# A twelve-stage fp32 transformer kernel on one core: later squares in the first stage, and layer norms that take the mean from a bank of its own

## The chip, the core and the metric

The kernel runs on one core of a Trainium2 chip. That core has TensorE (matrix products, PE in the rows), VectorE (DVE), ScalarE (ACT), GpSimd (POOL) and SyncE (SP), which here issues nearly all the transfers. Each engine works through a list of instructions of its own, in order, and semaphores connect the lists. The metric is the device time of one execution, in microseconds.

## The reference

A batch of one, 256 tokens, width 1024. The first block has two layers: gated feed-forward pieces (stages f0 to f3), a mixer (m0, m1) and a cross attention (c0, c1), each behind an RMS norm. The second block has two layers: a mixer (b0, b1), a feed-forward piece (f4, f5), and a layer norm behind each of them.

```python
def swiglu(h, w_gate, w_up, w_down):
    return (jax.nn.silu(h @ w_gate) * (h @ w_up)) @ w_down

mix = jnp.concatenate([o_gla, o_rwkv, o_nsa], axis=-1) @ w_out[l]
x = _layer_norm(DEEPNORM_ALPHA * x + mix, ln1_w[l], ln1_b[l])
ffn = (jax.nn.silu(x @ ffn_w_gate[l]) * (x @ ffn_w_up[l])) @ ffn_w_down[l]
x = _layer_norm(DEEPNORM_ALPHA * x + ffn, ln2_w[l], ln2_b[l])
```

## The kernel before, in words

The state x lies with its features on the partitions, as eight blocks k of 128 features by 256 tokens. Products are near fp32: every operand is split into a high part of the type fp32r and a rest. For a weight unit of 128x1024 (eight tiles of 128x128), ScalarE writes the high part `w_hi` (L148, `act_split`) and VectorE the rest `w_lo` (L159, `dve_split`); TensorE then runs, for each tile, a product of 512 columns with `w_hi` (high part and rest of the activations side by side) and one of 256 columns with `w_lo`. These two are called a pair below. Where the high part and the rest of the activations are multiplied apart there are three products of 256 columns, a triple.

Weights come through a ring of six slots (`ring`) and are split into four slots of `w_hi` and `w_lo`. A transfer waits until the slot's last unit has been split, a split until the unit four before it has been used by TensorE.

The order is written out by hand. Each stage has a list of pieces, and every engine goes through the same list and does its share of each piece (`pe_program`, `act_program`, `dve_program`, `pool_program`). Splits are put between the pieces: in `f` stages each unit as early as `can_split` allows, in the mixers where the strings of `WEAVE` have a dot (high part) or a comma (rest). In these strings z is a warm-up product (`pe_warm`: the identity times itself into an idle bank, result unused) and m the next piece of the output chain, with the layer norm at its end.

What the change touches:

- Stage f0. Pieces x0 to x8 make the high part and rest of the activations h (`act_x`, `dve_x`). GpSimd squares x and adds the squares up (`pool_x`: eight squares and six additions into `rows`). `pe_rs` sums them over the partitions (piece rs 0, products `ps<-consts,rows`), VectorE takes the root (`dve_rs`), and piece rs 1 spreads it over the partitions (`ps<-consts,stats`). Gate j of side h is eight pairs; the first one, j = 0, is done for both sides together, block by block. The column sums of rs 0 stand before its last block.
- The layer norm (`pe_ln`, `act_ln`, `dve_ln`, `pool_ln`, pieces from `ln_pieces`) is run behind b0, f4, b1 and f5. Piece x adds a block of the result, ld centres it by a mean over the first half (VectorE) and squares it (ScalarE), GpSimd adds the squares up. Piece ls sums x and the squares over the partitions into the two halves of one bank; ScalarE squares the mean, VectorE subtracts (`rows<-ps,rows`), ScalarE takes logarithm and exponential for the reciprocal root R, and VectorE writes the mean M (`scratch<-ps`). Piece lm subtracts M from blocks 0 and 1 on VectorE and from blocks 2 to 7 on GpSimd (`x<-x,scratch`). Piece lx multiplies a block by R (`x<-x,rows`), ScalarE writes the high part `h` with gain and bias and the new x, VectorE writes the rest (`h<-x,h`). For blocks 1, 4 and 7 (`vector_norm`) VectorE writes the new x. The next stage's first products need, block by block, the rest.

## Time and profile before

| | us |
|---|---|
| median of 3 runs | 2079.61 |
| lowest and highest run | 2076.35, 2083.39 |
| span of the profiled execution (first to last instruction) | 2076.2 |
| TensorE, matmuls busy | 1971.9 |
| VectorE busy | 1512.7 |
| ScalarE busy | 1117.3 |
| GpSimd busy | 408.7 |

The profiled execution has no time of its own beside its span; the fastest run is 0.15 us above that span, so what lies around the span is taken as small, and the median run is 3.4 us above it. Times within the trace count from the first instruction. A busy matmul time has modelled ends, since matmuls overlap.

### The profile page before, as it was taken

How to read it: one execution, taken by the hardware profiler on the slowest of the kernel's cores; microseconds unless marked ns; L12 is line 12 of the kernel's file. 1: busy time of each engine (PE TensorE's matmuls, PEld its weight loads, DVE VectorE, ACT ScalarE, POOL GpSimd, SP SyncE). 2: the span in 40 equal slices, each digit the busy share in tenths (PEclk: the TensorE clock that was granted, in tenths of full speed). 3: DMA queues.
4: the chain of work that ended last, by engine and by line, in shares of the span. 5: the costliest groups of instructions: out<-in, count | busy, mean ns of one | idle time of the engine just before them, and what ended most of it. 6: DMA issues, size and time to landing. Idle time of an engine off the chain costs nothing.

```text
span 2076.2 us, 32905 instructions
## 1 busy us (share of the span) xinstructions
PE 1971.9 (95%) x12512; PEld 1721.6 (83%) x12512; DVE 1512.7 (73%) x2649; ACT 1117.3 (54%) x2048; POOL 408.7 (20%) x371
## 2 busy tenths in 40 slices
PE   7999999999999999899999998899998999899997
PEld 6888888888888888698888977588887878688886
DVE  6976776787678767777876688577766687677765
ACT  5654565565455556655554543456554543456554
POOL 3521002222112210023220101102213012112213
PEclk9999999999999999999999998999999899999999
DMA  7556533355556555044555440225555240234652
GB/s 252 190 178 196 168 132 116 121 191 178 179 192 194 182 185 182 32 153 165 188 180 186 141 134 1 87 93 174 191 183 177 85 135 30 77 113 151 191 183 85
DMA packets 88718, 309.83 MB, mean 149 GB/s; under 512 B 9840, under 2 KB 11632, under 8 KB 88176
## 3 DMA queue, kind: packets, MB, share of 16 engines
q1 hardware_dynamic: 88272, 305.03, 44.9%
q10 hardware_dynamic: 288, 2.69, 0.4%
q8 instruction: 100, 1.64, 0.3%
q14 instruction: 58, 0.48, 0.1%
HBM read 306.63 MB, written 1.05 MB: 148 GB/s over the span
## 4 chain that ended last, share of the span: by engine, by line
PE 81%; DVE 10%; ACT 4%; issue 3%; POOL 1%; DMA 1%; SPq 0%; DVEq 0%; ACTq 0%; POOLq 0%
PE ps L134 79%; DVE scratch L159 3%; ACT scratch L148 2%; PE ps L139 2%; DVE w_lo L159 2%; DVE stats L176 1%; DVE scratch L165 1%; POOL rows L159 1%; DVE scratch L186 1%; DMA ring<-in_w 1%; ACT w_hi L148 1%; ACT L153 0%; DVE scratch L171 0%; DVE stats L159 0%; DVE x L159 0%
## 5 line engine op out<-in xcount | busy, mean ns | idle before, releaser
L134 PE MATMUL ps<-h,w_hi 128*128 128x512 f32 (+1 forms) x2912 | 900.2, 370 | 25.2 <-DVE w_lo L159 16.3
L159 DVE TENSOR_TENSOR w_lo<-ring,w_hi 128x1024 fp32r<-128x1024 f32 (+3 forms) x573 | 699.0, 1230 | 302.8 <-ACT w_hi L148 299.7
L148 ACT ACTIVATE w_hi<-ring 128x1024 fp32r<-128x1024 f32 (+3 forms) x573 | 584.3, 1029 | 419.3 <-PE ps L134 413.9
L134 PE MATMUL ps<-h,w_lo 128*128 128x256 f32 x2512 | 708.5, 282 | 0.0
L134 PEld LDWEIGHTS ps<-h,w_hi 128*128 128x128 f32 x2912 | 530.2, 192 | 124.3 <-issue 21.0
L134 PEld LDWEIGHTS ps<-h,w_lo 128*128 128x128 f32 x2512 | 481.3, 192 | 0.0
L134 PE MATMUL ps<-f,w_hi 128*128 128x512 f32 (+1 forms) x1444 | 417.7, 355 | 0.1
L134 PE MATMUL ps<-f,w_lo 128*128 128x256 f32 x1184 | 331.2, 280 | 0.0
L159 POOL TENSOR_TENSOR f<-f_work,f 128x256 fp32r<-128x256 f32 x132 | 185.1, 1403 | 557.4 <-ACT f L148 557.3
L134 PEld LDWEIGHTS ps<-f,w_hi 128*128 128x128 f32 x1444 | 254.4, 189 | 41.9 <-issue 0.4
L134 PEld LDWEIGHTS ps<-f,w_lo 128*128 128x128 f32 x1184 | 223.8, 189 | 0.1
L134 PE MATMUL ps<-scratch 128*128 128x128 f32 (+8 forms) x1696 | 200.1, 319 | 15.2 <-DVE scratch L159 7.1
L134 PEld LDWEIGHTS ps<-scratch 128*128 128x128 f32 (+3 forms) x1696 | 162.5, 181 | 50.7 <-issue 16.4
L185 ACT ACTIVATE scratch<-ps 128x512 f32<-128x512 f32 (+9 forms) x196 | 91.2, 485 | 188.2 <-PE ps L134 149.9
L159 POOL TENSOR_TENSOR rows<-x 128x256 f32<-128x256 f32 x64 | 52.8, 826 | 481.6 <-DVE x L159 472.4
L159 DVE TENSOR_TENSOR f_work<-f_work,ps 128x256 f32<-128x256 f32 x306 | 126.7, 415 | 6.7 <-ACT f_work L185 6.6
L159 DVE TENSOR_TENSOR f_work<-f_work 128x256 f32<-128x256 f32 x264 | 113.7, 431 | 8.6
L134 PE MATMUL ps<-w_hi,h 128*128 128x512 f32 (+2 forms) x384 | 112.5, 369 | 1.9 <-DVE w_lo L159 1.5
L185 ACT ACTIVATE f_work<-ps 128x256 f32<-128x256 f32 x306 | 111.2, 366 | 1.3 <-PE ps L134 1.3
L139 PE MATMUL ps<-consts,scratch 128*128 128x128 f32 (+3 forms) x428 | 70.1, 296 | 31.0 <-DVE scratch L165 14.9
L159 DVE TENSOR_TENSOR scratch<-scratch 128x512 f32<-128x512 f32 (+7 forms) x108 | 70.3, 678 | 35.3 <-ACT scratch L185 27.4
L148 ACT ACTIVATE scratch<-ps,stats 128x256 f32<-128x256 f32 (+3 forms) x143 | 68.9, 497 | 47.0 <-PE ps L134 25.1
(158 smaller groups left out, 2048.1 us busy)
## 6 DMA issues: line engine op xcount, KB each, us to landing
ring<-in_w SPq DMA_DIRECT2D x518, 512.0 KB, 3.8
ring<-in_w SPq DMA_DIRECT2D x48, 384.0 KB, 3.6
ring<-in_w SPq DMA_DIRECT2D x16, 396.0 KB, 3.2
ring<-in_w SPq DMA_DIRECT2D x8, 256.0 KB, 5.4
stage_consts<-in_ctwo ACTq DMA_DIRECT2D x1, 1346.0 KB, 6.2
stage_consts<-in_cthree ACTq DMA_DIRECT2D x1, 1283.0 KB, 5.7
x<-in_x SPq DMA_DIRECT2D x4, 256.0 KB, 6.9
scratch<-in_m SPq DMA_DIRECT2D x1, 1024.0 KB, 10.5
```

Source lines behind the costliest of these rows:

```text
L134: return self.e.matmul(out, lhsT, rhs, start=start, stop=stop, skip_group_check=free)
L139: return self.e.transpose(out, x, self.K.ident[0:x.shape[0], 0:x.shape[0]])
L148: return self.e.activation(out, x, func, **k)
L159: return self.e.tensor_tensor(out, a, b, op)
L165: return self.e.tensor_scalar(out, a, s1, None, op0)
L176: return self.e.tensor_reduce(out, a, AX, op, negate=negate)
L185: return self.e.activation(out, a, ACT.Copy)
L186: return self.e.tensor_copy(out, a)
```

## The change

First stage: the four transfers of x are issued by ScalarE ahead of everything, beside SyncE's constants and weights. The first four weight units now hold both sides of two blocks each (before: one side of four blocks), and the pieces x, high split and rest split alternate. Seven warm-up products run before the first gate (before, the nine of the list found no idle bank and none was issued). GpSimd starts its squares only when all of h is ready, and rs 0 and rs 1 come two blocks later: rs 0 behind gate (2, 1), rs 1 behind gate (3, 0). A table load of ScalarE moves to the start. In f1, f2 and f3 the column sums stand behind the last block of the first gates, no longer ahead of it.

Layer norms: the sum of x has a bank of its own (`lmean`) and its own signal, so ScalarE squares the mean while the squares are still being summed. GpSimd's six subtractions go to VectorE, each right behind a multiplication by R. VectorE writes the new x of blocks 0, 2, 4 and 6, and ScalarE copies its high part. In b0 and b1 the rest splits ahead of the last blocks move behind them (the strings `WEAVE`, of which the diff shows a line), and f4 has no rest split behind its last product. The warm-up products are 12 behind the sums in b0 and b1, and 16 ahead of the next stage's first product behind f4 (12 of f4 and the 4 with which b1 begins; before 4).

```diff
-           ".,znzzuvzzmmmm,mm.m...,,m,mmmm.mmm,mmmm.m,mmzm,mzmmzmmzzzzzzmmmzmmmzzzzzzmmzm"),
+           ".,znzzuvzzmmmm,mm.m...,,m,mmmm.mmmmmmmm.mmmmmm,mzzzzzzzzzzzzmmmmm,,mmmmm"),
...
-        b = K.bank(e, ring, (s, "ls"))
+        b = [K.bank(e, OUT if s[0] == "b" else ring, (s, "lmean")), K.bank(e, ring, (s, "ls"))]
...
-            ins = e.mm(b[:, 256 * n:256 * n + 256], K.onec.broadcast_to([128, 128]), k, i == 0, i > len(sums) - 3, free=True)
-        ins.then_inc(*e.up("summed", (s, "ls")))
+            ins = e.mm(b[n][:, 0:256], K.onec.broadcast_to([128, 128]), k, start, i == end[n])
+            if i == end[n]:
+                ins.then_inc(*e.up("summed", (s, ("lmean", "ls")[n])))
...
-    return AFTER[s] != "out" and i % 3 == 1
+    return AFTER[s] != "out" and i % 2 == 0
...
-        b = K.psum((s, "ls"))
-        e.wait_ge(*K.at("summed", (s, "ls")))
-        e.act(K.R, b[:, 0:256], ACT.Square, scale=1.0 / D).then_inc(*e.up("ln_mean_squares", s))
-        e.wait_ge(*K.at("ln_variance", s))
+        e.wait_ge(*K.at("summed", (s, "lmean")))
+        e.act(K.R, K.psum((s, "lmean"))[:, 0:256], ACT.Square, scale=1.0 / D).then_inc(*e.up("ln_mean_squares", s))
+        e.wait_ge(*K.at("evicted", (s, "ls")))
         e.then(e.act(K.R, K.R, ACT.Ln, bias=ln_eps(K)))
         e.act(K.R, K.R, ACT.Exp, scale=-0.5).then_inc(*e.up("ln_rstd", s))
     elif what == "lx" and i < 8:
         w, b = (c[:, i:i + 1] for c in ln_columns(K, s))
-        e.wait_ge(*K.at("ln_scaled", (s, i)))
         x = K.x[:, i, :]
-        if AFTER[s] != "out":
-            e.act(K.h_hi[:, i, :], x, ACT.Identity, scale=w, bias=b).then_inc(*e.up("split_hi", (AFTER[s], i)))
-        if not vector_norm(s, i):
+        if vector_norm(s, i):
+            e.wait_ge(*K.at("normed", (s, i)))
+            e.cp(K.h_hi[:, i, :], x).then_inc(*e.up("split_hi", (AFTER[s], i)))
+        else:
+            e.wait_ge(*K.at("ln_scaled", (s, i)))
+            if AFTER[s] != "out":
+                e.act(K.h_hi[:, i, :], x, ACT.Identity, scale=w, bias=b).then_inc(*e.up("split_hi", (AFTER[s], i)))
             e.act(x, x, ACT.Identity, scale=w, bias=b).then_inc(*e.up("normed", (s, i)))
 
 
...
         e.wait_ge(*K.at("ln_mean_squares", s))
-        b = K.psum((s, "ls"))
-        e.stt(K.R, b[:, 256:512], 1.0 / D, K.R, MUL, SUB).then_inc(*e.up("ln_variance", s))
-        e.then(e.ts(M, b[:, 0:256], 1.0 / D, None, MUL), "evicted", (s, "ls"))
+        e.wait_ge(*K.at("summed", (s, "ls")))
+        e.stt(K.R, K.psum((s, "ls"))[:, 0:256], 1.0 / D, K.R, MUL, SUB).then_inc(*e.up("evicted", (s, "ls")))
+        e.ts(M, K.psum((s, "lmean"))[:, 0:256], 1.0 / D, None, MUL).then_inc(*e.up("evicted", (s, "lmean")))
     elif what == "lm":
-        for k in range(2):
-            e.tt(x[:, k, :], x[:, k, :], M, SUB).then_inc(*e.up("ln_shifted", (s, k)))
+        for k in range(SHIFTED):
+            dve_shift(e, K, s, k)
     elif what == "lx":
         if i < 8:
             e.wait_ge(*K.at("ln_rstd", s))
             e.wait_ge(*K.at("ln_shifted", (s, i)))
             e.tt(x[:, i, :], x[:, i, :], K.R, MUL).then_inc(*e.up("ln_scaled", (s, i)))
+            if i + SHIFTED < 8:
+                dve_shift(e, K, s, i + SHIFTED)
+            if vector_norm(s, i):
+                w, b = (c[:, i:i + 1] for c in ln_columns(K, s))
+                e.wait_ge(*K.at("ln_scaled", (s, i)))
+                e.ts(x[:, i, :], x[:, i, :], w, b, MUL, ADD).then_inc(*e.up("normed", (s, i)))
         if i and AFTER[s] != "out":
             k = i - 1
-            if vector_norm(s, k):
-                w, b = (c[:, k:k + 1] for c in ln_columns(K, s))
-                e.wait_ge(*K.at("split_hi", (AFTER[s], k)))
-                e.then(e.ts(x[:, k, :], x[:, k, :], w, b, MUL, ADD), "normed", (s, k))
+            e.wait_ge(*K.at("split_hi", (AFTER[s], k)))
             e.wait_ge(*K.at("normed", (s, k)))
             e.tt(K.h_lo[:, k, :], x[:, k, :], K.h_hi.bitcast(F32)[:, k, :], SUB).then_inc(*e.up("split_x", (AFTER[s], k)))
+
+
+SHIFTED = 2
+
+
+def dve_shift(e, K, s, k):
+
+    e.wait_ge(*K.at("evicted", (s, "lmean")))
+    x, M = K.x[:, k, :], ln_area(K)[3]
+    e.tt(x, x, M, SUB).then_inc(*e.up("ln_shifted", (s, k)))
 
 
 def pool_ln(e, K, s, what, i):
...
-    elif what == "lm":
-        e.wait_ge(*K.at("evicted", (s, "ls")))
-        for k in range(2, 8):
-            e.tt(x[:, k, :], x[:, k, :], M, SUB).then_inc(*e.up("ln_shifted", (s, k)))
...
-    return p + [("ls", 0), ("lm", 0)] + [("lx", i) for i in range(9)]
+    warm = [("warm", 0)] * (12 if s == "f4" else 0)
+    return p + [("ls", 0)] + warm + [("lm", 0)] + [("lx", i) for i in range(9)]
...
-        out = [] if self.stage != "f0" else ([("warm", 0)] * 9 + x_order(range(2)) + hi + x_order((2,)) + lo + x_order(range(3, 6))
-                                             + hi + x_order((6,)) + lo + x_order((7, 8)))
+        hi, lo, x = [("split_hi", 0)], [("split_lo", 0)], lambda *js: x_order(js)
+        out = [] if self.stage != "f0" else (
+            [("warm", 0)] * 7 + x(0) + hi + x(1) + lo + x(2) + hi + x(3) + lo + x(4) + hi + x(5) + lo + x(6) + hi + x(7) + lo + x(8))
...
+                out += gate(2, 0, ("sum", (1, 0))) + gate(2, 1, ("sum", (1, 1)), ("rs", 0))
+                out += gate(3, 0, ("sum", (2, 0)), ("rs", 1), ("scale", 0))
...
-        per = 4 if (s, j) == ("f0", 0) else 8
...
+            u = [K.unit(e, True, [tile(h, k) for k in (k0, k0 + 1) for h in halves]) for k0 in (0, 2, 4, 6)]
...
-                if (h, k) == (0, 7) and not F.second:
-                    pe_rs(e, K, ALL8, s, 0)
...
+        if i == 0:
+            e.wait_ge(*K.at("split_x", (s, 7)))
...
-    for b in K.idle_banks(e)[0:1]:
+    for b in (K.idle_banks(e) if K.holder else [K.ps[7]])[0:1]:
...
+    for i in range(4):
+        e.dma(K.x[:, 2 * i:2 * i + 2, :], K.XD[:, 2 * i:2 * i + 2, :]).then_inc(K.S.sem("loaded_x%d" % i), 16)
+    e.sigmoid_table()
...
-                dve_splits(e, K, early and (name, what) != ("f0", "x"))
+                last = name == "f4" and (what, i) in (("down", (7, 2)), ("x", 7))
+                dve_splits(e, K, early and not last and (name, what) != ("f0", "x"))
```

Where the instructions stand now. VectorE in the first stage, from the rest splits of gates (2, 0) and (2, 1) to the first step of the root (`stats<-ps`), with what each waits for; before:

```order
L159 TENSOR_TENSOR w_lo<-ring,w_hi 128x1024 [waits split_hi_act,loaded4,unit_used_pe]
L159 TENSOR_TENSOR w_lo<-ring,w_hi 128x1024 [waits split_hi_act,loaded5,unit_used_pe]
L159 TENSOR_TENSOR w_lo<-ring,w_hi 128x1024 [waits split_hi_act,loaded0,unit_used_pe]
L159 TENSOR_TENSOR w_lo<-ring,w_hi 128x1024 [waits split_hi_act,loaded1,unit_used_pe]
L166 TENSOR_SCALAR stats<-ps 128x2 [waits summed_pe]
L165 TENSOR_SCALAR stats<-stats 128x2 [waits evicted_dve]
```

and now:

```order
L164 TENSOR_TENSOR w_lo<-ring,w_hi 128x1024 [waits split_hi_act,loaded1,unit_used_pe]
L164 TENSOR_TENSOR w_lo<-ring,w_hi 128x1024 [waits split_hi_act,loaded2,unit_used_pe]
L164 TENSOR_TENSOR f_work<-f_work,ps 128x256 [waits copied_act]
L164 TENSOR_TENSOR w_lo<-ring,w_hi 128x1024 [waits split_hi_act,loaded3,unit_used_pe]
L164 TENSOR_TENSOR f_work<-f_work,ps 128x256 [waits copied_act]
L164 TENSOR_TENSOR w_lo<-ring,w_hi 128x1024 [waits split_hi_act,loaded4,unit_used_pe]
L164 TENSOR_TENSOR f_work<-f_work,ps 128x256 [waits copied_act]
L164 TENSOR_TENSOR w_lo<-ring,w_hi 128x1024 [waits split_hi_act,loaded5,unit_used_pe]
L164 TENSOR_TENSOR f_work<-f_work,ps 128x256 [waits copied_act]
L171 TENSOR_SCALAR stats<-ps 128x2 [waits summed_pe]
L170 TENSOR_SCALAR stats<-stats 128x2 [waits evicted_dve]
```

Behind the same splits stand four more of them and four additions of gate sums (`f_work<-f_work,ps`) before the root begins.

VectorE behind the last blocks of b0; `rows<-ps,rows` is the variance, `scratch<-ps` is M, `x<-x,scratch` subtracts M, `x<-x,rows` multiplies by R, `h<-x,h` writes the rest that TensorE waits for. Before, from the split between blocks 6's and 7's work:

```order
L159 TENSOR_TENSOR w_lo<-ring,w_hi 128x1024
L171 SCALAR_TENSOR_TENSOR x<-ps,x 128x256
L171 SCALAR_TENSOR_TENSOR x<-x,ps 128x256
L171 SCALAR_TENSOR_TENSOR x<-ps,x 128x256
L171 SCALAR_TENSOR_TENSOR rows<-ps,rows 128x256
L165 TENSOR_SCALAR scratch<-ps 128x256
L159 TENSOR_TENSOR x<-x,scratch 128x256 x2
L159 TENSOR_TENSOR x<-x,rows 128x256 x2
L159 TENSOR_TENSOR h<-x,h 128x256
L159 TENSOR_TENSOR x<-x,rows 128x256
L166 TENSOR_SCALAR x<-x,consts 128x256
L159 TENSOR_TENSOR h<-x,h 128x256
```

and now, from the subtraction for block 3 to the multiplication of block 4 and beyond:

```order
L164 TENSOR_TENSOR x<-x,rows 128x256
L164 TENSOR_TENSOR x<-x,scratch 128x256
L164 TENSOR_TENSOR h<-x,h 128x256
L164 TENSOR_TENSOR x<-x,rows 128x256
L164 TENSOR_TENSOR x<-x,scratch 128x256
L171 TENSOR_SCALAR x<-x,consts 128x256
L164 TENSOR_TENSOR h<-x,h 128x256
L164 TENSOR_TENSOR x<-x,rows 128x256
L164 TENSOR_TENSOR x<-x,scratch 128x256
L164 TENSOR_TENSOR h<-x,h 128x256
L164 TENSOR_TENSOR w_lo<-ring,w_hi 128x1024 x2
L164 TENSOR_TENSOR x<-x,rows 128x256
```

A pair of weight splits stands between the rest of block 2 and the multiplication of block 4, and every multiplication is followed by a subtraction that was GpSimd's.

TensorE at the end of f4, from the last two sums (`ps<-x,consts` and `ps<-scratch,consts`) to the first triple of b1; before:

```order
L134 MATMUL ps<-scratch,consts 128x256 x2
L134 MATMUL ps<-x,consts 128x256
L134 MATMUL ps<-scratch,consts 128x256
L134 MATMUL ps<-consts 128x128 x4
L134 MATMUL ps<-h,w_hi 128x256 x2
L134 MATMUL ps<-h,w_lo 128x256
```

and now:

```order
L134 MATMUL ps<-scratch,consts 128x256 x2
L134 MATMUL ps<-x,consts 128x256
L134 MATMUL ps<-scratch,consts 128x256
L134 MATMUL ps<-consts 128x128 x16
L134 MATMUL ps<-h,w_hi 128x256 x2
L134 MATMUL ps<-h,w_lo 128x256
```

The warm-up products are sixteen instead of four; nothing else moved there.

## Rows read from the trace of the kernel before

**Rows 1.** The page's first part: busy us, share of the span, instructions.
```profile
PE 1971.9 (95%) x12512; PEld 1721.6 (83%) x12512; DVE 1512.7 (73%) x2649; ACT 1117.3 (54%) x2048; POOL 408.7 (20%) x371
```

**Rows 2.** Timeline of the first stage: start, us, engine, line, operation, [idle before <-releaser].
```profile
13.93 1.06 ACT L148 ACTIVATE w_hi<-ring 128x1024 fp32r<-128x1024 f32 x1 [0.42 <-DMA ring<-in_w]
16.19 0.68 POOL L159 TENSOR_TENSOR rows<-x 128x256 f32<-128x256 f32 x1
16.31 3.29 DVE L159 TENSOR_TENSOR w_lo<-ring,w_hi 128x1024 fp32r<-128x1024 f32 x2
18.60 1.47 POOL L159 TENSOR_TENSOR rows<-x 128x256 f32<-128x256 f32 x1
20.13 1.59 PE L134 MATMUL ps<-consts,rows 128*128 128x1 f32 x8 [3.29 <-POOL rows L159]
30.74 1.06 ACT L148 ACTIVATE w_hi<-ring 128x1024 fp32r<-128x1024 f32 x1 [1.44 <-PE ps L134]
...
33.51 1.06 ACT L148 ACTIVATE w_hi<-ring 128x1024 fp32r<-128x1024 f32 x1 [1.44 <-PE ps L134]
```

**Rows 3.** Busy time by window: us, PE, PEld, DVE, ACT, POOL, PEclk, DMA share, GB/s.
```profile
23.00:27.80 4.80, 4.80 (x18) 4.08 (x18) 3.73 (x11) 1.61 (x2) 0.00 (x0) 0.55 0.41 137
```

**Rows 4.** Timeline of POOL, 60 to 72 us, within the gates of f0.
```profile
59.62 12.94 POOL L159 TENSOR_TENSOR scratch<-scratch 128x256 f32<-128x256 f32 x12
```

**Rows 5.** Timeline at the start of f3.
```profile
958.77 1.05 PE L134 MATMUL ps<-consts,rows 128*128 128x1 f32 x8 [0.99 <-POOL rows L159]
```

**Rows 6.** Timeline of the layer norm behind b0.
```profile
1399.85 1.73 DVE L171 SCALAR_TENSOR_TENSOR x<-ps,x 128x256 f32<-128x256 f32 x5
...
1401.20 3.22 POOL L159 TENSOR_TENSOR scratch<-scratch 128x256 f32<-128x256 f32 x3 [2.36 <-ACT scratch L148]
...
1404.48 1.56 PE L134 MATMUL ps<-scratch,consts 128*128 128x256 f32 x6
...
1413.14 0.76 PE L134 MATMUL ps<-h,w_hi 128*128 128x512 f32 x1 [2.11 <-issue]
```

**Rows 7.** Timeline of the layer norm behind f4.
```profile
1599.91 1.23 DVE L159 TENSOR_TENSOR w_lo<-ring,w_hi 128x1024 fp32r<-128x1024 f32 x1 [0.92 <-ACT w_hi L148]
1601.05 0.41 DVE L171 SCALAR_TENSOR_TENSOR x<-x,ps 128x256 f32<-128x256 f32 x1
...
1603.58 0.42 DVE L171 SCALAR_TENSOR_TENSOR rows<-ps,rows 128x256 f32<-128x256 f32 x1 [1.65 <-ACT rows L148]
...
1604.48 5.22 POOL L159 TENSOR_TENSOR x<-x,scratch 128x256 f32<-128x256 f32 x6 [7.94 <-DVE scratch L165]
...
1605.58 1.80 DVE L159 TENSOR_TENSOR x<-x,rows 128x256 f32<-128x256 f32 x2
...
1608.35 0.77 PE L134 MATMUL ps<-h,w_hi 128*128 128x256 f32 x2 [4.33 <-issue]
```

**Rows 8.** Busy time by window, behind b0 and behind f4.
```profile
1415.00:1417.00 2.00, 2.00 (x9) 1.75 (x8) 1.51 (x6) 1.56 (x4) 0.00 (x0) 0.62 0.00 0
1612.00:1614.00 2.00, 2.00 (x11) 2.00 (x11) 1.93 (x6) 1.63 (x4) 0.00 (x0) 0.50 0.00 0
```

**Rows 9.** Timeline of the layer norm behind b1.
```profile
1866.10 3.23 POOL L159 TENSOR_TENSOR scratch<-scratch 128x256 f32<-128x256 f32 x3 [2.17 <-ACT scratch L148]
...
1872.50 3.73 PE L134 MATMUL ps<-consts 128*128 128x128 f32 x32
1873.12 0.42 DVE L171 SCALAR_TENSOR_TENSOR rows<-ps,rows 128x256 f32<-128x256 f32 x1 [1.79 <-ACT rows L148]
...
1877.90 0.47 PE L134 MATMUL ps<-h,w_hi 128*128 128x512 f32 x1 [1.66 <-issue]
```

**Rows 10.** Timeline of the last layer norm, behind f5.
```profile
2065.44 0.42 DVE L171 SCALAR_TENSOR_TENSOR rows<-ps,rows 128x256 f32<-128x256 f32 x1 [1.65 <-ACT rows L148]
...
2071.88 2.07 ACT L148 ACTIVATE x<-x,consts 128x256 f32<-128x256 f32 x4 [0.27 <-DVE x L159]
```

**Rows 11.** Instructions on the tile rows: duration ns min/median/max, first and last start.
```profile
L159 DVE TENSOR_TENSOR x<-x,rows x32: 411/420/951, 1410.4 to 2072.4; 128x256 f32<-128x256 f32 x32
```

More of the change, by code:

```diff
@@ L148, in act, with sigmoid_table @@
         return self.e.activation(out, x, func, **k)
+    def sigmoid_table(self):
+        if self.e is not None:
+            self.e.preload_act_table_set("sigmoid_and_others")
     def exp_ln_table(self):
@@ L796, in pe_ln @@
         sums += [(1, sq)] + [(n, k) for k in range(4, 8) for n in range(2) if k > first and (n or k > 5 or s[0] == "f")]
+        end = [max(i for i, x in enumerate(sums) if x[0] == n) for n in range(2)]
         for i, (n, k) in enumerate(sums):
+            start = i == min(m for m, x in enumerate(sums) if x[0] == n)
             if k is dev or k is sq:
@@ L1008, in pe_ffn @@
     elif what == "rs":
-        if i:
-            pe_rs(e, K, ALL8, s, i)
+        pe_rs(e, K, ALL8, s, i)
     elif what == "mem":
@@ L3580, in sp_program @@
 def sp_program(e, K):
-    before = {0: (0,), 2: (1, 2), 4: (3,)}
     for u in K.units:
-        for i in before.get(u.n, ()):
-            e.dma(K.x[:, 2 * i:2 * i + 2, :], K.XD[:, 2 * i:2 * i + 2, :]).then_inc(K.S.sem("loaded_x%d" % i), 16)
         if u.n == 0:
@@ L3606, in build @@
     K.begin(True)
+    K.XD = nc.dram_tensor("in_x", [128, 8, 256], F32, kind="ExternalInput").ap()
     K.CD = {a: K.Cs[:, 0:1] for a in K.ncol}
```

63 lines of the change are left out of this document (38 added, 25 removed).

## The prediction

> **What bounds the kernel.** I read the page's first part, the waits of TensorE, then the timeline around each place that the change touches. TensorE is busy for 1971.9 of 2076.2 us [rows 1], so a part of the change counts only where TensorE waits or runs at its lower clock. In the first stage it waits 3.29 us for GpSimd's squares and then runs at a granted clock of 0.55 until 27.8 us [rows 2, 3]; in f3 it waits 0.99 us for them [rows 5]. Behind b0, f4 and b1 it waits for a layer norm that passes between four engines, and behind f5 the norm is the program's tail [rows 6, 7, 9, 10]. Everywhere else it runs without a gap that the edits reach, and what is gained or lost at these places moves the rest with it.
>
> **Layer norm behind f4, the largest term.** Before: VectorE was idle from 1598.99, began a weight split at 1599.91, and only behind it added the last block, at 1601.05, though the last product had ended at about 1598.7. That split now stands behind the block. So the block starts at about 1598.95: 2.1 us. The sum of x now has its own signal: ScalarE's square of the mean (the 0.4 us step before 1603.58) lies beside the last sum of squares: 0.4 us. Then, from the variance to TensorE's first product, 4.77 us (1603.58 to 1608.35). Its two multiplications by R took 1.80 us while GpSimd subtracted M for 5.22 us [rows 7]; over all 32 such instructions the median is 0.42 us and the longest 0.95 [rows 11]. With GpSimd's subtractions gone I price VectorE's instructions at 0.35 us from start to start, as five went by in 1.73 us [rows 6]. Counted from the variance: M at 0.35, subtractions 0.8 and 1.15, R ready at 1.42 (0.51 and 0.42 us on ScalarE behind the variance), multiply 1.5, subtract 1.8, new x 2.15, multiply 2.6, subtract 2.9, and the rest of block 0, for which ScalarE has copied the high part by 3.0, from 3.3 to 3.7. TensorE starts at 3.8 instead of 4.8: 1.0 us. Together the first product comes 3.5 us earlier, 1604.9. I bound this from both sides: nothing of the last step if the instructions stay at 0.9 us, 3.5 as reckoned.
>
> The clock there: TensorE stood still for 4.33 us, and its first products behind it ran at 0.50, still so in 1612 to 1614 [rows 7, 8]; the window that ends it is about 1614.2, so 5.9 us at half speed did 2.95 us of work. Sixteen warm-up products now fill the gap: 32 products took 3.73 us behind b1 [rows 9], as many half-products as these sixteen make, against a gap of 3.9. Behind b1 the same filling kept the clock through 1.66 us of waiting. I take 2.9 us. From here on VectorE must give a block each 1.44 us (TensorE's pace at the full clock) and needs 3.5 instructions, 1.2 us: it holds. Sum for f4: 6.3 us; bounds 2.5 and 6.5.
>
> **Behind b0.** The two splits between the last blocks go behind them, so these do not hold anything; but the bound was another: GpSimd's additions of the squares, 3.22 us for three, slowed by VectorE's split beside them, then TensorE's sums from 1404.48 and the first product at 1413.14 [rows 6]. At 0.75 each the additions end at 1403.5, 0.95 earlier (they still start at 1401.2 behind ScalarE's weight split). Seven sums at 0.43 to 0.5 us are 3.1, then 3.8 as above: first product at 1410.3, 2.85 earlier. Against that: two weight splits, 2.4 us, now stand between the rest of block 2 and block 4's multiplication, which also holds back the rest of block 3. By the same count the rest of block 3 is ready 9.9 us behind the variance, and TensorE, at full clock 1.39 us a block, wants it at 8.0: a new wait of 2.0 us. Before, half clock until about 1416.4, 0.62 in 1415 to 1417 [rows 8], cost 1.6 us, which is saved if twelve warm-up products hold it. Sum: 2.85 + 1.6 - 2.0 = 2.4 us; bounds -0.5 (the new wait brings the clock down too, and the norm is no faster) and 4.5.
>
> **Behind b1.** GpSimd's three additions took 3.23 us from 1866.10 [rows 9]; without the split beside them 2.3: 0.95, and 0.3 from closer sums; the mean's own bank 0.4, and 1.0 from the variance on. The clock was full already. One split stands in the middle: a wait of 0.9 us, about as long as the 0.7 us that TensorE waited there before for block 1. Sum 2.4 us; bounds 0.5 and 3.5.
>
> **Behind f5.** The bank gives 0.4. From the variance at 2065.44 to the end of ScalarE's last block at 2073.95 are 8.5 us [rows 10]. Now VectorE needs two instructions a block: eight multiplications and eight subtractions from 0.8 to 6.3, and the last block on ScalarE 0.6: 6.9. Sum 2.0 us; bounds 0.4 and 2.2.
>
> **First stage.** SyncE's fifth weight unit, the first of gate (1, 0), lands at 13.93 [rows 2], and in both kernels all of x, the constants and four smaller units are ahead of it. I keep that time, so h is complete at about 14.4 and, with a split on ScalarE (1.06) and one on VectorE (1.65), gate (1, 0) starts at 16.6. In these rows the transfer could come up to 1.9 us earlier, the time SyncE spent on issuing x; I give that no value.
>
> The Trainium skill, DMA: Bandwidth & Descriptors, section Issuing engines are not separate DMA queues, says that transfers started by several engines run on the same 16 DMA engines and that a second issuer saves only sequencer time. By it the landing at 13.93 stands; if instead the earlier issue counted in full, the sum would grow by 1.9 us.
>
> Four gates of 2.78 us (30.74 to 33.51 is one [rows 2]) end at 27.7. That is where rs 0 now stands. But GpSimd starts its fourteen operations only at 14.4. Beside VectorE's weight splits it took 1.47 us for one and VectorE 3.29 for two; without them 0.68 [rows 2]. The first is done at 15.1; beside the next four splits (6.6 us) four more; the remaining nine go at the pace of twelve in 12.94 us between gates [rows 4], 9.7 us. The squares are ready at 31.4, and TensorE waits 3.7 us, about as long as it did before, and like then comes out at half clock. Column sums 1.4, gate (3, 0) at half clock 5.3 and rs 1 0.5 end at 38.6; VectorE's root (2.4 us) lies beside that gate. Before, gate (1, 1) ended at 30.7, and (2, 0), rs 1, (2, 1) and (3, 0) at 39.4. Gain 0.8 us: the wait is moved, not removed. Bounds: -1.5 (splits hold GpSimd longer) and 6.5 (next part). What is queued behind this wait: nothing but gate (3, 0); VectorE's fourth split, root and sums wait as well, but its splits are four units ahead.
>
> **f1 to f3.** The column sums stand two pairs (0.7 us) later; of f3's wait that hides at most 0.7, in f1 and f2 nothing waits. I take 0.6; bounds 0 and 0.7. The table load that ScalarE does earlier lies beside waits; seven warm-up products run while TensorE waits for x: nothing.
>
> **The sum.** 6.3 + 2.4 + 2.4 + 2.0 + 0.8 + 0.6 = 14.5 us, from a span of 2076.2 to 2061.7. The median run is 3.4 above the span, so 2079.6 - 14.5 = 2065.1; I say 2065.
>
> **Rivals.**
> - The squares come in time. GpSimd at 0.82 us an operation, as it goes beside small VectorE work, needs 11.5 us and is done at 25.9, ahead of 27.7. Then TensorE has no wait: gates to (2, 1) at 27.7, sums 1.0, gate (3, 0) to 31.5, rs 1 behind the root at about 33.3, against 39.4: 6.1 us instead of 0.8, total 19.8, 2060. For it: ScalarE and DMA may hold the splits back, which leaves GpSimd alone; against it the 1.47 us and the twelve in 12.94.
> - The layer norms give half. The new wait behind b0 comes with idle time ahead of it and brings the clock down (1.6 us lost, 1.6 not saved), and sixteen products behind f4 do not keep the clock (2.9 not gained); 14.5 - 6.1 = 8.4, 2071. For it: 2.11 us of standing still were enough behind b0 [rows 6]; against it the 1.66 of rows 9.
> - Slower: VectorE becomes the norm's bound. It takes over six subtractions a norm. If its instructions with two operands stayed at 0.90 us, the two of rows 7, without GpSimd beside them, the rest of block 0 would come eight instructions behind M, at 8.0 instead of 3.7, and every block at 3.15 us, 1.76 above TensorE's pace: 4.3 + 12.3 = 16.6 us more than reckoned in each of three norms, and 16 x 0.55 = 8.8 in the last, 59 in all against 14.5 gained: 2124. It decides from about 0.5 us an instruction on, where the losses eat the gain. Against it: the median of 0.42 with starts 0.35 apart [rows 6, 11].
>
> **Chances and range.** Forecast 0.52, squares in time 0.22, half 0.17, slower by VectorE 0.03; 0.06 for what I do not see, of which a third slower. About 0.3%, 6.2 us, is what a measurement of this kernel can tell from no change. Faster by more: nearly all of the first two, three quarters of the third, 0.86; within 0.3% 0.09; slower 0.05. The range takes in the second case and the third: 2056 to 2073; the forecast's own is 2061 to 2069.
>
> **What would show it.** First stage: the wait ahead of the column sums at about 28 us (3 to 4.5 us, released by GpSimd) with half clock behind it; if it is under 1 us, the first rival holds. VectorE's `x<-x,rows` at a median and maximum near 0.42. Behind f4: last block added within 0.4 us of the last product, 3.8 us from variance to the first product, clock 1.00 behind it. Behind b0: a wait of about 2 us for block 3's rest. GpSimd's six subtractions gone from the tail, and 7 us from the last variance to ScalarE's end. The forecast is wrong if the norms save less than 9 us together, or if a stage that the edits do not touch changes by over 1 us.

## The result, and the profile after

| | before | changed |
|---|---|---|
| median of 6 runs each, us | 2080.11 | 2066.39 |
| lowest to highest | 2072.41 to 2083.39 | 2061.96 to 2070.72 |
| profiled execution, us (span) | 2079.61 (2076.2) | 2063.89 (2062.1) |
| ratio, 95% interval | | 0.9936 [0.9912, 0.9961] |

The forecast was 2065 in 2056 to 2073. Timed again (e11) the ratio was 0.9950 [0.9933, 0.9966], so the two intervals together reach from 7 to 18 us gained. One of e2's twelve runs took 2759.68 us, with a mean granted clock of 0.65 where the others had 0.98, and is left out below. The page's first part: TensorE is busy for as long as in [rows 1], in a shorter span.

```profile
PE 1971.9 (96%) x12528; PEld 1717.9 (83%) x12528; DVE 1505.7 (73%) x2676; ACT 1112.6 (54%) x2044; POOL 388.9 (19%) x347
```

First stage, timeline of the changed kernel (start, us, engine, line, operation, idle before and its releaser), against [rows 2]; helper lines are 5 higher than before:

```profile
11.73 2.11 ACT L148 ACTIVATE w_hi<-ring 128x1024 fp32r<-128x1024 f32 x2
12.85 2.17 POOL L164 TENSOR_TENSOR rows<-x 128x256 f32<-128x256 f32 x2 [12.41 <-DVE h L176]
14.60 0.50 PE L134 MATMUL ps<-h,w_hi 128*128 128x512 f32 x1 [0.23 <-DVE w_lo L164]
...
29.47 0.61 POOL L164 TENSOR_TENSOR rows<-x 128x256 f32<-128x256 f32 x1
30.14 1.87 PE L134 MATMUL ps<-consts,rows 128*128 128x1 f32 x8 [4.17 <-POOL rows L164]
```

ScalarE splits the fifth weight unit at 11.73, 2.2 us earlier than the 13.93 that the forecast kept. It did not wait for it: the unit's semaphore shows that it landed at 11.41, and before at 13.85. Gate (1, 0) starts at 14.60. The squares end at 30.08, and the wait for them is 4.17 us. Behind it the clock is at its lower level until about 36 (by window: us, PE busy, PEclk, DMA share, GB/s):

```profile
33.00:35.00 2.00, 2.00 (x8) 0.50 0.00 0
37.00:39.00 2.00, 2.00 (x15) 1.00 0.00 0
```

Behind b0, against [rows 6]:

```profile
1396.68 2.37 POOL L164 TENSOR_TENSOR scratch<-scratch 128x256 f32<-128x256 f32 x3 [2.33 <-DVE x L176]
1402.50 0.42 DVE L176 SCALAR_TENSOR_TENSOR rows<-ps,rows 128x256 f32<-128x256 f32 x1 [1.99 <-PE ps L134]
1406.31 0.47 PE L134 MATMUL ps<-h,w_hi 128*128 128x512 f32 x1 [1.24 <-DVE h L164]
1408.30 2.36 DVE L164 TENSOR_TENSOR w_lo<-ring,w_hi 128x1024 fp32r<-128x1024 f32 x2
1412.04 0.50 PE L134 MATMUL ps<-h,w_hi 128*128 128x512 f32 x1 [1.33 <-DVE h L164]
```

GpSimd's three additions take 2.37 us instead of 3.22, the first product comes 3.81 us behind the variance, and the new wait for block 3, behind the two splits at 1408.30, is 1.33 us. Behind f4, against [rows 7]:

```profile
1595.40 0.41 DVE L176 SCALAR_TENSOR_TENSOR x<-x,ps 128x256 f32<-128x256 f32 x1
1596.33 0.70 PE L134 MATMUL ps<-x,consts 128*128 128x256 f32 x2 [0.28 <-DVE x L176]
1597.32 3.73 PE L134 MATMUL ps<-consts 128*128 128x128 f32 x32
1597.59 0.43 DVE L176 SCALAR_TENSOR_TENSOR rows<-ps,rows 128x256 f32<-128x256 f32 x1
1601.24 0.47 PE L134 MATMUL ps<-h,w_hi 128*128 128x256 f32 x2 [0.19 <-issue]
...
1615.90 0.51 PE L134 MATMUL ps<-h,w_hi 128*128 128x256 f32 x2 [2.91 <-DVE w_lo L164]
```

TensorE waits 0.28 us for the last block (2.43 before), then the warm-up products reach to its first product, 3.65 us behind the variance. Behind b1 and f5, against [rows 9, 10], and the view of the tile rows, against [rows 11]:

```profile
1852.91 2.36 POOL L164 TENSOR_TENSOR scratch<-scratch 128x256 f32<-128x256 f32 x3 [2.17 <-ACT scratch L148]
1858.72 0.42 DVE L176 SCALAR_TENSOR_TENSOR rows<-ps,rows 128x256 f32<-128x256 f32 x1 [1.95 <-PE ps L134]
1862.53 0.47 PE L134 MATMUL ps<-h,w_hi 128*128 128x512 f32 x1 [1.24 <-DVE h L164]
...
2052.51 0.42 DVE L176 SCALAR_TENSOR_TENSOR rows<-ps,rows 128x256 f32<-128x256 f32 x1 [1.31 <-PE ps L134]
2054.64 5.12 ACT L148 ACTIVATE x<-x,consts 128x256 f32<-128x256 f32 x8 [0.71 <-DVE x L164]
```

```profile
L164 DVE TENSOR_TENSOR x<-x,rows x32: 417/422/429, 1404.0 to 2058.5; 128x256 f32<-128x256 f32 x32
```

The longest multiplication by R is 429 ns; before it was 951.

**How the places are compared.** The two spans differ by 14.1 us, but not all of the difference comes from the edits. In the feed-forward stages TensorE went at one of two paces, 0.3467 or 0.3533 us for a pair of products of w_hi and w_lo, with the granted clock at 1.00 in both. It shows in VectorE's splits, since five gates lie between such rows. Before and changed, f1:

```profile
454.62 1.23 DVE L159 TENSOR_TENSOR w_lo<-ring,w_hi 128x1024 fp32r<-128x1024 f32 x1 [0.36 <-ACT w_hi L148]
468.75 1.23 DVE L159 TENSOR_TENSOR w_lo<-ring,w_hi 128x1024 fp32r<-128x1024 f32 x1 [0.71 <-ACT w_hi L148]
```

```profile
450.40 1.23 DVE L164 TENSOR_TENSOR w_lo<-ring,w_hi 128x1024 fp32r<-128x1024 f32 x1 [0.30 <-ACT w_hi L148]
464.27 1.22 DVE L164 TENSOR_TENSOR w_lo<-ring,w_hi 128x1024 fp32r<-128x1024 f32 x1 [0.67 <-ACT w_hi L148]
```

14.13 against 13.87 us: f1 is 2.8 us shorter (190.0 to 187.2) and f2 3.0 us longer (184.9 to 187.9), and all that the edits do there is to place the column sums two pairs later. The kernel before was slow in f1, f3 and in f0 up to about 88 us, the changed one in f2, f4 and f5. So a gain is read below from a short stretch around its place, between the same two instructions in each trace. The first four of them repeated within 0.05 us in two reruns of the changed kernel (e1, e11). The end of f5 is taken as the span, rounded to 0.1 us.

| stretch | before | changed | gain | forecast |
|---|---|---|---|---|
| f4: block 6 added to first product behind b1's wait for w_lo | 32.10 | 25.80 | 6.30 | 6.3 |
| b0: block 4 added to f4's second gate sum | 32.13 | 30.09 | 2.04 | 2.4 |
| b1: block 5 added to f5's first gate sum | 26.34 | 24.07 | 2.27 | 2.4 |
| f5: last block added to the end | 13.29 | 11.78 | 1.51 | 2.0 |
| f3, at the slower pace (changed: e1) | 190.64 | 189.93 | 0.71 | 0.6 |
| f0: start to last gate sum (before: e3, most of it at the faster pace) | 144.30 | 142.94 | 1.4 | 0.8 |

Sum 14.2, forecast 14.5. The row of f0 is the least certain: in eight traces with the first stage's edits and the sums behind gate (2, 1) the last gate sum stands at 142.15 to 144.17, in the two traces without them at 144.30 and 145.81.

That the spans differ by 14.1 as well is chance. Outside these places b1's attention (from f4's variance to b1's first blocks) was 7.2 us shorter (253.39 to 246.19), f1 and, by its pace, f3 about 3 us shorter each, f2 and the gates of f4 and f5 about 3 us longer each, b0's attention 1.4 longer (248.79 to 250.18). So the forecast's own last sign of being wrong, a stage that the edits do not touch changing by over 1 us, did come. e1 shows changes of that size between two executions of one program, so the sign could not tell the forecast's errors from such changes.

### The profile page after: what moved, and what is told of

It is laid out like the page before. It is cut to its first block, busy times and chain, and to the rows that moved or that the text cites. A ratio compares the mean times of both kernels' runs of the same rounds, so it can differ in the third digit from the quotient of the medians.

```text
span 2062.1 us, 32965 instructions
## 1 busy us (share of the span) xinstructions
PE 1971.9 (96%) x12528; PEld 1717.9 (83%) x12528; DVE 1505.7 (73%) x2676; ACT 1112.6 (54%) x2044; POOL 388.9 (19%) x347
## 4 chain that ended last, share of the span: by engine, by line
PE 80%; DVE 11%; ACT 4%; issue 2%; POOL 2%; DMA 1%; SPq 0%; DVEq 0%; ACTq 0%; POOLq 0%
PE ps L134 78%; DVE scratch L164 3%; ACT scratch L148 2%; DVE w_lo L164 2%; PE ps L139 2%; POOL rows L164 1%; DVE scratch L170 1%; DVE stats L181 1%; DMA ring<-in_w 1%; DVE scratch L191 1%; ACT w_hi L148 1%; DVE x L164 1%; ACT L158 1%; DVE scratch L176 0%; POOL scratch L164 0%
## 5 line engine op out<-in xcount | busy, mean ns | idle before, releaser
L134 PEld LDWEIGHTS ps<-h,w_hi 128*128 128x128 f32 x2912 | 524.3, 190 | 113.1 <-issue 7.9
L134 PE MATMUL ps<-scratch 128*128 128x128 f32 (+8 forms) x1696 | 205.6, 325 | 14.7 <-DVE scratch L164 7.1
```

Source lines behind the costliest of these rows:

```text
L134: return self.e.matmul(out, lhsT, rhs, start=start, stop=stop, skip_group_check=free)
```

## The experiments

Times beside before are ratios of the runs on the same chip. "Changed" is the changed kernel. Where four stretches are given, they are those of b0, f4, b1 and f5. e1 and e5 to e9 have one run each: 2072.65, 2077.54, 2067.61, 2084.29, 2071.22 and 2063.77 us, with 2082.62 for one run of the kernel before beside e5 to e8. One run shows no gain of this size by its time, so these are read in their traces.

**e1, the changed kernel again**, no edit.

> The changed kernel once more, with nothing edited. In its first trace TensorE took 0.3467 us for a pair of products of w_hi and w_lo in f0, f1 and f3 and 0.3533 us in f2, f4 and f5; in the kernel before it was 0.3533 in f1, f3 and the first 50 us of f0 and 0.3467 in f2, f4 and f5. That is up to 3 us a stage, as much as one term of the forecast. If the pace belongs to the program, this trace has it at the same stages again and the per-place gains read from the two traces are off by it for a reason of the change. If it is drawn anew in each execution, at least one stage changes its pace here, and it is noise to be taken out of every comparison of two traces. Places that don't hang on it should repeat within 0.3 us: GpSimd's wait of 4.2 us ahead of the column sums, 3.8 us from variance to first product behind b0, 3.65 behind f4, 3.8 behind b1. Span 2060 to 2066.

2072.65 us, span 2070.9, above the 2060 to 2066 expected: 8.8 us more than the first trace of the same program. f3 went at the slower pace here, at the faster in the first:

```profile
994.38 1.22 DVE L164 TENSOR_TENSOR w_lo<-ring,w_hi 128x1024 fp32r<-128x1024 f32 x1 [0.66 <-ACT w_hi L148]
...
1008.50 1.22 DVE L164 TENSOR_TENSOR w_lo<-ring,w_hi 128x1024 fp32r<-128x1024 f32 x1 [0.35 <-ACT w_hi L148]
```

14.12 us for five gates; in the first trace it was 13.86 at the same place (992.82 to 1006.68). f3 took 189.93 instead of 186.98. And b1's attention, from f4's variance to the add of b1's blocks 0 and 1, took 251.5 instead of 246.2. So for f1 and f3 the pace is drawn anew in each execution of one program: f1 was fast, fast and slow in the three traces of the changed kernel (first, e1, e11), f3 fast, slow and slow. For f2 this is not shown. It was slow in all twelve traces that have the first stage's edits and fast in the two that have not (before, e3), 187.9 against 184.9 us. With so few traces it may be chance, or these edits cost 3.0 us there. The places repeated: 30.07, 25.79, 24.05 and 11.82 us; only the squares' wait was 3.40 instead of 4.17, outside the 0.3 I had allowed.

**e2, the first stage's edits alone** (kernel before with the changes to `order`, `pe_ffn`, the loads of x, GpSimd's wait and the table load).

> The kernel before with the first stage's edits alone (loads of x from ScalarE's queue, units of two blocks, squares behind the last block, column sums of f0 two gates later, weights of one gate together in f1 to f3, the early table load); the layer norms as before. By the two traces the first stage and f3 gave 1.9 + 0.8 = 2.7 us once the pace is taken out: 2077.4, and 4.77 and 4.3 us behind f4 as before. By the forecast's own terms 1.4: 2078.7. If the first stage gave what the raw positions say (2.9 by the end of f0, 5.9 by the end of f3), 2074.

Median of the eleven runs 2082.30, ratio 1.0011 [0.9995, 1.0028]: from 1.0 us faster to 5.8 us slower. The 2.7 us faster that were expected are outside that, and the forecast's own 1.4 too. In the trace f0's last gate sum is at 143.33, 0.4 later than in the changed kernel, and f3 takes 189.93; the two places gave 1.0 and 0.7. f2 took the slower pace, which would more than undo both (before, then e2):

```profile
672.43 1.23 DVE L159 TENSOR_TENSOR w_lo<-ring,w_hi 128x1024 fp32r<-128x1024 f32 x1 [0.66 <-ACT w_hi L148]
686.29 1.23 DVE L159 TENSOR_TENSOR w_lo<-ring,w_hi 128x1024 fp32r<-128x1024 f32 x1 [0.30 <-ACT w_hi L148]
```

```profile
673.15 1.22 DVE L164 TENSOR_TENSOR w_lo<-ring,w_hi 128x1024 fp32r<-128x1024 f32 x1 [0.35 <-ACT w_hi L148]
687.28 1.22 DVE L164 TENSOR_TENSOR w_lo<-ring,w_hi 128x1024 fp32r<-128x1024 f32 x1 [0.71 <-ACT w_hi L148]
```

13.86 and 14.13 us for five gates. Norms as before: 32.12 and 26.50 us at b0 and b1. At f4 it is 30.81 instead of 32.10, since the half clock behind the wait was 1.3 us cheaper: so much can the clock's part of [rows 7, 8] vary.

**e3, the layer norms' edits alone.**

> The kernel before with the layer norms' edits alone (mean's own bank, subtractions on VectorE, norms by turns, twelve warm-up products behind f4, the splits behind the last sums), the first stage as before. By the traces b0 gave 2.0, f4 6.4, b1 2.3 and f5 1.5: 12.2 us, 2067.9. By the forecast 13.1: 2067. If the two parts of the change feed one another (a norm that starts earlier finds its weights later), this and the first-stage part don't add to the whole 13.7.

Median 2066.18, ratio 0.9927 [0.9904, 0.9951]: 10 to 20 us, as much as the whole change's gain, with 2067 to 2067.9 expected. The four stretches: 30.07, 25.81, 23.95, 11.58. f3 took 189.20 here at the faster pace, against 186.98 in the changed kernel: behind its wait of 0.98 us for the squares the granted clock was 0.81 in 955 to 960 and 0.85 in 960 to 965, while it stayed at 1.00 in the kernel before. So later column sums can be worth up to 2.2 us in f3 and not only 0.7.

**e4, column sums of f0 two gates later.**

```
-  gate(2, 1, ("sum", (1, 1)), ("rs", 0))
-  gate(3, 0, ("sum", (2, 0)), ("rs", 1), ("scale", 0))
-  gate(3, 1, ("root", 0), ...)
+  gate(2, 1, ("sum", (1, 1)))
+  gate(3, 0, ("sum", (2, 0)))
+  gate(3, 1, ("sum", (2, 1)), ("sum", (3, 0)), ("rs", 0))
+  gate(4, 0, ("sum", (3, 1)), ("rs", 1), ("scale", 0), ("root", 0), ("scale", 1), ("prod", 0))
```

> The changed kernel with f0's column sums behind gate (3, 1) instead of (2, 1), and R, scale, root and product 0 behind (4, 0). Theory: the 4.17 us wait for GpSimd's squares (they end at 30.1) and the half clock from 31.9 to 36 behind it are all that is left of the first stage's loss; with two more gates (5.6 us) ahead of the sums, from 25.9 to 31.5, the wait is gone and the clock stays full: 4.2 + about 2 = 6 us gained at the end of f0. Rival: the wait only moves on, because VectorE, which is already behind (its sums trailed TensorE until 111 us), gets its root, scale and products 2.8 us of TensorE's time later and TensorE then waits for a bank or a weight split at gate (5, 0) or (6, 0): gain 0 to 2 us, with a new wait on w_lo or ps between 40 and 60 us.

The sums start at 31.53 without a wait, and the clock stays at 1.00. TensorE's remaining waits in this stretch:

```profile
37.19 0.68 PE L134 MATMUL ps<-consts,stats 128*128 128x128 f32 x4 [1.79 <-DVE stats L176]
...
52.24 0.50 PE L134 MATMUL ps<-h,w_hi 128*128 128x512 f32 x1 [0.50 <-DVE w_lo L164]
```

The last gate sum is at 139.89, 3.1 us earlier than in the changed kernel, with the slower pace from 80 us on (60 us at 1.9% are 1.1), so 4.2 of the expected 6. The 1.79 us for R took the rest. With e10 and e12 there are three traces with these later sums, at 139.89 to 140.61, all below the eight at 142.15 to 144.17. The median, 2068.3 (ratio 0.9942 [0.9922, 0.9962]), doesn't show it.

**e5, no extra warm-up products behind f4**: `[("warm", 0)] * (0 if s == "f4" else 0)`.

> The changed kernel without the twelve extra warm-up products behind f4 (four are left). Read from the last block but one of f4 to TensorE's first product behind its 2.91 us wait in b1, which was 32.10 us before and 25.80 with the change. Theory (forecast): the warm-ups hold the clock through the 3.65 us from variance to first product; without them about 3 us of it TensorE stands still, the first products run at half clock for some 6 us and 2.5 to 3 us are lost: 28.5 us. Rival: 3.65 us of which four warm-ups fill 0.5 is too short to bring the clock down, or the wait behind it absorbs the loss: 25.8 to 26.3.

```profile
1605.63 1.05 PE L134 MATMUL ps<-consts 128*128 128x128 f32 x8
1609.55 0.77 PE L134 MATMUL ps<-h,w_hi 128*128 128x256 f32 x2 [2.86 <-issue]
```

```profile
1610.00:1612.00 2.00, 2.00 (x11) 0.50 0.00 0
```

28.44 us, where 28.5 was expected: the warm-ups are worth 2.64.

**e6, a split ahead of f4's last block**: the rule `last` out of `dve_program`.

> The changed kernel with the rule 'last' taken out, so VectorE may again split a weight ahead of f4's last block. Theory: the last block is added behind a split (1.2 us and what it waits for), about 2.1 us after the last product instead of at once, and the stretch from the last block but one to the first product behind b1's 2.91 us wait grows from 25.8 by 2.1 to 27.9; the split itself was taken out of nothing that anybody waited for. Rival: the split that is taken back out of the norm's tail shortens b1's 2.91 us wait for w_lo by up to 1.2, and only 0.9 is lost: 26.7.

```profile
1595.22 0.70 PE L134 MATMUL ps<-x,consts 128*128 128x256 f32 x2 [2.43 <-DVE x L176]
...
1596.31 5.27 PE L134 MATMUL ps<-consts 128*128 128x128 f32 x32
```

The wait is 2.43 again, as before, and 2.15 of the 3.34 us lost (29.14, with 27.9 expected) are that; the rest is clock, since here the sums and warm-ups behind the wait ran at 0.52 in 1596 to 1598 (32 products 5.27 us instead of 3.73, and the first product 4.71 us behind the variance instead of 3.65). b1's wait for w_lo stayed 2.91, against the rival.

**e7, GpSimd subtracts M from blocks 2 to 7** (`pool_ln` does it again, `dve_ln` no longer).

```
     elif what == "lm":
+        for k in range(SHIFTED, 8):
+            e.tt(x[:, k, :], x[:, k, :], M, SUB)...
-            if i + SHIFTED < 8:
-                dve_shift(e, K, s, i + SHIFTED)
```

> The changed kernel with GpSimd subtracting M from blocks 2 to 7 again (VectorE only 0 and 1), everything else as changed. Theory: it is GpSimd's work beside it that made VectorE's multiplications by R 0.90 us; they are 0.7 to 0.95 again while GpSimd subtracts (5.2 us), and variance to first product goes from 3.65 (f4) and 3.81 (b0, b1) back to about 4.7; behind f5, from the variance to the end of the span 9.6 us become about 11, since ScalarE waits for blocks that GpSimd gives at 0.87 us each. Rival: the order of VectorE's instructions and the earlier M did it, and GpSimd's subtractions cost nothing: 3.65 and 3.8 stay, with blocks at 0.42 us, and the tail gets shorter, since VectorE has half the work there.

```profile
1608.33 5.11 POOL L164 TENSOR_TENSOR x<-x,scratch 128x256 f32<-128x256 f32 x6 [5.45 <-DVE scratch L170]
1609.44 0.94 DVE L164 TENSOR_TENSOR x<-x,rows 128x256 f32<-128x256 f32 x1
1611.04 0.94 DVE L164 TENSOR_TENSOR x<-x,rows 128x256 f32<-128x256 f32 x1
```

```profile
L164 DVE TENSOR_TENSOR x<-x,rows x32: 410/419/948, 1412.7 to 2078.3; 128x256 f32<-128x256 f32 x32
```

Variance to first product is 5.52 us at f4 and 5.66 at b0, the stretches are 31.59, 29.15, 26.92 and 13.02 us: 8.9 us more than changed in the four norms. At b0, f4 and b1 the first product is 1.9 us later, and the clock falls to 0.50 behind it. That is 0.8 us worse than the 4.7 expected and than the kernel before: beside GpSimd's subtractions the new order of VectorE's work is worse than the old. The cause of the slow multiplications is shown: the same instruction takes 0.42 us, and 0.94 while GpSimd subtracts.

The Trainium skill, SBUF — State Buffer, section SBUF: two separate sides, says that a VectorE operation with two operands in SBUF and a GpSimd operation that reads SBUF hold their shared ports one at a time for a whole instruction. The trace fits it: 0.94 is the 0.42 and about as much again, and GpSimd's six take 0.85 us each. VectorE's adds of blocks out of PSUM stay at 0.41 us even beside GpSimd's additions.

**e8, the old order of splits and warm-ups at the ends of b0 and b1**, norms as changed.

> The changed kernel with the old order of splits and warm-ups at the ends of b0 and b1, the norms' own code as changed. Stretches from the add of block 4 to the second gate sum of the next stage: b0 32.13 before, 30.09 with the change; b1 (block 6 to f5's first sum) 26.34 and 24.07. Theory (forecast): the splits beside GpSimd's additions cost 0.95 at b0 and b1, which come back, but the 1.33 us wait for block 3 at b0 and 0.20 at b1 go: b0 29.8 to 30.5, b1 24.9. Rival: the old order was as good at b0 and worse at b1 by the full 0.95 + 0.3: b0 29.5, b1 25.3. If the marks gave most of the gain at b0: over 31.

b0 29.42, b1 24.56, both a little below what was expected (29.8 to 30.5 and 24.9), b0 where the rival had it (29.5). The expectation calls b1's mark block 6; it is block 5, as in the table. At b0 the way to the variance is 1.01 us longer than changed (three additions 3.21 us again), but from the first product on it is 1.67 shorter, without the two splits in the middle. So the new order of splits is a loss of 0.67 at b0 and a gain of 0.49 at b1.

**e9, squares as soon as x is loaded**: GpSimd's wait for `split_x` of block 7 removed.

> The changed kernel with GpSimd's wait for the last block's split taken out: it squares each block of x as soon as it is loaded, while VectorE splits x and the first weights. Theory: the fourteen operations then start at about 6 instead of 12.9 us; they and VectorE's splits slow one another (1.5 us an operation beside a split), so they end at about 24, ahead of the column sums at 25.9; the 4.17 us wait and the half clock behind it go, but h and the first splits come later and gate (0, 0) ends 1 to 3 us later: f0's last gate sum 2 to 5 us earlier than 142.9. Rival: the delay on VectorE is as long as the whole overlap (7 operations or more beside x's splits at double time), gates (0, *) end 4 us later or more and nothing is gained at f0's end, 142 to 144.

```profile
4.58 1.56 POOL L164 TENSOR_TENSOR rows<-x 128x256 f32<-128x256 f32 x2 [4.14 <-DMA x<-in_x]
7.56 1.71 DVE L176 SCALAR_TENSOR_TENSOR h<-x,consts,h 128x256 fp32r<-128x256 f32 x2
10.34 0.50 PE L134 MATMUL ps<-h,w_hi 128*128 128x512 f32 x1 [0.19 <-DVE w_lo L164]
16.39 0.68 POOL L164 TENSOR_TENSOR rows<-x 128x256 f32<-128x256 f32 x1
```

The squares end at 17.07 and nothing waits for them at 29.61; VectorE's pairs of splits of x take 1.71 us instead of 0.88, and gate (1, 0) starts at 18.20 instead of 14.60. TensorE then waits 1.50 us for R at 34.94, for which nothing was reckoned. Last gate sum 141.06: 1.9 us gained, just under the 2 to 5 expected, in one trace.

**e10, three moves**: e4's, the split `,` behind the norm's block 3 of b0 moved ahead of its variance, and b1's first two splits ahead of the evictions.

```
-  b0 "...mmmmmm,mzzzzzzzzzzzzmmmmm,,mmmmm"   b1 "zzzzr.,r,.r..,,..."
+  b0 "...mmmmmm,,mzzzzzzzzzzzzmmmmm,mmmmm"   b1 "zzzz.,.,rrr..,,..."
```

> Sums of f0 behind gate (3, 1), as in the run before, and two moves of splits: behind b0 one of the two splits in the middle of the norm stands ahead of the variance, where VectorE waits 1.99 us for the last sums; in b1 the first two splits of weights stand ahead of the evictions of the first receptance products on both engines, so they run while TensorE still multiplies. Theory: 4 us at f0; at b0 the 1.33 us wait for block 3 becomes 0.2: 30.09 to 29.0; in b1 the 2.91 us wait for w_lo and the half clock behind it (about 2 us) go: 4 to 5 us. Sum 9 us under the changed kernel, about 2057. Rivals: at b0 the split ahead of the variance comes in the way of it (GpSimd's additions or the variance 0.5 later), no gain; in b1 the weights' DMA lands too late for it, and the wait only shrinks to 1.5 us.

Median 2063.35, ratio 0.9915 [0.9888, 0.9942], the lowest of the medians, though about 2057 was expected. f0's last gate sum is at 140.61. b0's stretch is 28.94, the wait for block 3:

```profile
1408.67 0.50 PE L134 MATMUL ps<-h,w_hi 128*128 128x512 f32 x1 [0.20 <-DVE h L164]
```

In b1 it failed. The wait came one group of products later, as the next splits now stood behind ScalarE's eviction of that group, and the way to the first product on stage_consts was 38.43 us instead of 37.63:

```profile
1615.42 0.60 ACT L190 ACTIVATE scratch<-ps 128x512 f32<-128x512 f32 x1 [5.16 <-PE ps L134]
1616.05 0.69 DVE L164 TENSOR_TENSOR scratch<-scratch 128x512 f32<-128x512 f32 x1 [3.19 <-ACT scratch L190]
1618.85 0.80 PE L134 MATMUL ps<-h,w_hi 128*128 128x256 f32 x2 [3.25 <-DVE w_lo L164]
```

**e11, the changed kernel again, timed beside e10.**

> The changed kernel unedited, timed beside the former on the same chip: 2066 median, spread 2060 to 2073, since the pace of each feed-forward stage is drawn anew (each of six stages 2.5 to 3 us longer or not).

Ten runs, 2067.91 to 2075.50, median 2069.83, where 2066 in 2060 to 2073 was expected, ratio 0.9950 [0.9933, 0.9966]; stretches 30.07, 25.78, 24.06, 11.76.

**e12, e10 with b1's splits as changed and eleven warm-up products in front of its wait** (`zzzzr.,r,.` + 11 `z` + `r..,,`).

> The changed kernel with three edits: column sums of f0 behind gate (3, 1); behind b0 one of the two splits ahead of the variance; in b1 eleven warm-up products where TensorE waits 2.91 us for w_lo, and the splits there left alone. Theory: 3 to 4 us at f0's end; b0's stretch 28.94 as measured before; in b1 the clock stays full behind the wait, and from the first product behind it to the next wait it takes 9.5 us, the shortest seen, instead of 11 to 12: 1.5 to 2.5. Sum 6 to 7 us, 2061 to 2063 against 2068 of the changed kernel over all its runs. Rival for b1: the clock falls for something other than this wait, and it stays at 11; or the eleven products outlast it and delay the next ones by up to 0.5.

```profile
1615.24 2.62 PE L134 MATMUL ps<-consts 128*128 128x128 f32 x22
1618.32 0.51 PE L134 MATMUL ps<-h,w_hi 128*128 128x256 f32 x2 [0.46 <-DVE w_lo L164]
```

```profile
1618.00:1622.00 4.00, 3.69 (x30) 1.00 0.39 134
```

The clock stays full, and to the next wait it is 9.49 us as expected, against 10.99 in the changed kernel. But in e7 and e8 it was 9.48 behind the unfilled 2.91 us wait too, so one trace does not show that the warm-up products did it. b0 28.93, f0's last sum 140.40. By these places 5.2 us are gained on the changed kernel (2.5, 1.2, 1.5); the median is 2066.82, above the 2061 to 2063 expected, ratio 0.9941 [0.9919, 0.9963], which overlaps with e11's. e10 and e12 beat the kernel before. That they beat the changed one is shown at their places in f0 and b0; by the times it is not shown for e12, and for e10 the intervals overlap by a little (0.9888 to 0.9942 against 0.9933 to 0.9966), with medians 6.5 us apart on one chip.

## Why the prediction was right

**f4, 6.3 forecast, 6.30 measured.** By its steps: the last block without a split ahead, 2.1, was 2.15 (e6 brings the 2.43 us wait back); the mean's own bank, 0.4, was 0.34; variance to first product, 1.0, was 1.12 (4.77 to 3.65), and e7 shows that it needs GpSimd's absence; the clock, 2.9, is the remainder of 2.69, and e5 gives 2.64. Added up, the forecast's four steps are 6.4 and not 6.3. That the total came out to the hundredth is luck: e2, with the norm as before, lost 1.3 less to the clock there, and against its 30.81 the gain is 5.0.

**b0, 2.4 forecast, 2.04 measured.** Up to the variance 1.37 were gained where 1.85 were reckoned: the additions gave 0.85 instead of 0.95, and the sums did not close up as far as I took it. From the variance 0.97 for 1.0. The clock saved less the new wait was -0.3 for -0.4. e8 has neither and parts the two: from the first product on the kernel before took 1.38 us more than e8, for 1.6 reckoned, and the changed one 1.67 more, for 2.0. The wait itself was 1.33.

**b1, 2.4 forecast, 2.27 measured**: 1.21 up to the variance (1.65 reckoned), 0.97 from it, 0.1 behind it.

**f5, 2.0 forecast, 1.51 measured.** The bank 0.34. From the variance to ScalarE's end 7.25 us instead of 6.9, since ScalarE's eight blocks take 0.64 each behind a first one at 2.13, not VectorE's pace and one block more: the term was 0.4 too large because I let VectorE set the end.

**First stage, 0.8 forecast, 1.4 measured, and the mechanism was the one forecast**: the wait for the squares is moved, not removed (4.17 against 3.7), with half clock behind it. One step was wrong. I kept the landing of the fifth unit at 13.93; it was 11.41, with the split at 11.73, and gate (1, 0) started at 14.60 instead of 16.6. Over all traces the unit landed at 13.85 and 13.20 without the first stage's edits (before, e3) and at 11.04 to 11.96 with them, 1.2 to 2.8 us earlier. The 1.9 that SyncE no longer spends on issuing x are of that size; no run has this edit alone. Nor is the early gate the landing's doing alone: with the unit there at 11.65 to 11.96 it started at 15.98 to 16.30 in e1, e2, e6 and e12, where TensorE had waited 0.6 to 1.3 us near 8.5 and, in e1, got through 8 products in 10 to 12 us instead of 14. The forecast gave the seven warm-up products nothing; whether they are what brings these gates forward, no run tested. The Trainium skill, DMA: Bandwidth & Descriptors, section Issuing engines are not separate DMA queues, says that a second issuer saves only the time on the sequencer, usually small against the transfer itself. The trace fits the first half, as the unit was issued at 3.29 instead of 4.96. Here that time was not small, and by reading the rule as no gain I kept a landing that moved. Because TensorE then came to the sums 1.7 us earlier than reckoned while the squares ended only 1.3 earlier, little of it was left. The 1.4 against 0.8 decides nothing, as the gate sums of equal edits lie 2 us apart.

**The rivals.** The squares did not come in time: GpSimd's fourteen operations took 17.2 us (17.0 reckoned). The norms did not give half: warm-ups held the clock at both places. VectorE did not become the bound: its multiplications by R stayed at 0.43 or below.

**What stays open.** The sum of the places is 14.2, the times say 7 to 18. That the first stage's edits bring anything to the whole is not shown: by e2's times they gain at most 1.0 us, less than its two places gave, and the norms alone (e3, 2066.18) were no slower than the whole change. f2's slower pace would explain it, and only more traces with and without these edits would tell. e2's b0 attention (f3's last block to b0's first) took 252.3 us against 248.8 and 248.0 in the two traces without these edits; in the twelve traces with them it was 246.5 to 253.7, so it may be chance. Nor is it known what sets TensorE's pace.
